# Feed-forward first layer by one level of Strassen's method, in an unrolled schedule of three groups

## The chip, the cores and the metric

The kernel runs on one core of a Trainium2 chip. Times are microseconds on the device; the metric is the median over several runs of the whole program. The profile is one further execution with the hardware profiler on.

## The reference

The reference computes one layer of a hybrid decoder in float32 for 512 prompt tokens and 32 sample tokens (544 in all, 1024 features):

```python
x = x + 0.5 * swiglu(rms_norm(x, norm_gain[l, 0]), ffn_in[l, 0], ffn_out[l, 0])
mix, st = token_mixer(rms_norm(x, norm_gain[l, 1]), ...)      # attention, pooling, caches
x = x + mix @ w_out[l]
x = x + 0.5 * swiglu(rms_norm(x, norm_gain[l, 2]), ffn_in[l, 1], ffn_out[l, 1])

def swiglu(h, w_io, w_o):
    gate, up = jnp.split(h @ w_io, 2, axis=-1)
    return (jax.nn.silu(gate) * up) @ w_o
```

`ffn_in` is 1024 x 5632 for each block: 22 tiles of 128 hidden features for the gate and as many for the up part. `ffn_out` is 2816 x 1024. The change touches these two feed-forward blocks. What lies between them (the projection with `w_in`, attention, pooling, the cache outputs, `w_out`) is computed as before.

## The kernel before, in words

Activations lie transposed: features on the partitions, the 544 tokens in the free dimension, in two halves of 272 (`HALF`). To keep float32 precision every operand of a product is split into a high part (`fp32r`, written by ScalarE with a Copy) and a low part (the remainder, a subtraction on VectorE), and `three(out, a, b)` issues three matmuls into one PSUM bank: high x high, high x low, low x high (lines 828 to 833).

A feed-forward block (`ffn(f)`, written once per engine) runs in two blocks of 11 tiles of hidden features (`BCH`). For each tile, `chunk` multiplies gate and up weights (two slots of the ring of four) with both halves of the tokens: 2 x 2 banks, 8 steps of k, 3 matmuls, 96 in all. Two sets of four banks alternate. ScalarE splits the next weights (`lead`, line 1313), applies silu to the gate banks (L1377) and writes the high part of the hidden tile (L1381); VectorE writes the weights' remainder (`remain`, L1647), multiplies silu by the up banks (L1744) and writes the hidden tile's remainder (L1734). After 11 tiles the second layer follows: 8 chunks of 128 output features, each 2 halves x 11 hidden tiles x 3 = 66 matmuls; VectorE adds half of the result to `XT` (L1763). The tiles run in hardware loops (`Fori`) on every engine.

What sets the order: each engine has its own list of instructions, written by hand, and waits on counting semaphores. `w_hi`, `w_lo` and `w_used` count weights split and weights consumed; SP loads weights into the ring when `w_used` says that a slot is free. Ahead of the first tile VectorE forms the normalised operands in pieces of 272 (`hn`, L1717, L1721), ScalarE their high parts (`parts`, L1362); TensorE begins with the first piece. In the second block of `ffn(0)` VectorE also prepares norm 1 after each chunk (L1771, L1630, L1631, L1775, L1777). GpSimd's list gathers cache pages, then issues 33 copies of cache rows from DRAM to DRAM, paced by `w_used` (L673), then computes the pooling windows (`windows`, L460 to L474) and later gathers again. It does no arithmetic in the feed-forward blocks.

Of the kernel before, what the change touches and what calls it, by code (L numbers as in the profile page):

```python
# [21 lines left out]
P = 128  # L22
# [140 lines left out]
def build(nc, I, O):  # L163
    ctx = ExitStack()
    with ctx:
# [27 lines left out]
        HIDH = put("HIDH", [P, BCH, T], "BIG", dt=F32R)  # L193
        HIDL = put("HIDL", [P, BCH, T], "BIG", BCH * T, dt=F32R)
# [44 lines left out]
        HIDF = BIG[:, BCH * T:2 * BCH * T].rearrange("p (n t) -> p n t", n=BCH)  # L239
# [23 lines left out]
        ff = [{n: sem(f"ffn{f}_{n}") for n in ("silu", "free", "mul", "hi", "lo")} for f in range(2)]  # L263
# [39 lines left out]
        CKS = CKT[:, :, :].rearrange("p b n -> p (b n)")  # L303
# [37 lines left out]
        MX1 = SM[:, 198:201]  # L341

# [141 lines left out]
        def _(sp):  # L484
# [14 lines left out]
            def chunk_loads(f, first, c, used):  # L499

                src = I["ffn_in"][0, f].rearrange("(k p) n -> p k n", p=P)
                for gs in range(2):
                    sl = (first + gs) % RING
                    if used is not None:
                        sp.wait_ge(w_used, used + gs)
                    dst = RAW[:, sl, 0:KD * P].rearrange("p (k n) -> p k n", k=KD)
                    sp.dma_start(dst, src[:, :, bass.ds(c * P + gs * FF, P)]).then_inc(landed[sl], 16)

            def ffn_loads(f):
                for blk in range(2):  # L510
# [20 lines left out]
                    src = I["ffn_out"][0, f].rearrange("(k p) n -> p k n", p=P)[:, blk * BCH:(blk + 1) * BCH, :]
                    for oc in range(KD):
                        sl = (L + oc) % RING
                        sp.wait_ge(w_used, L + oc - RING + 1)
                        sp.dma_start(RAW[:, sl, :].rearrange("p (k n) -> p k n", k=BCH),
                                     src[:, :, oc * P:(oc + 1) * P]).then_inc(landed[sl], 16)
# [109 lines left out]
        def _(pool):  # L646
# [24 lines left out]
            for dst, src, before in pieces:  # L671
                pool.wait_ge(w_used, 4 + 66 * before // copied)
# [59 lines left out]
            for b in range(2, NB):  # L732
                pool.wait_ge(sa["pva"], b - 1)
                load_slc(b)


        @block.tensor
        def _(pe):
# [102 lines left out]
            def ffn(f):  # L841
                pe.sem_inc(ff[f]["free"], 2)
                r = rs[2 * f]
                for blk in range(2):
                    L0 = L_FFN[f] + blk * L_BLOCK
                    e0 = blk * (BCH + KD)

                    def chunk(m, it, step):

                        L, e = L0 + 2 * m, e0 + m  # L850
                        pe.wait_ge(ff[f]["free"], it * step + (e + 1))
                        for hf in range(2):
                            for gs in range(2):
                                if hf == 0:
                                    pe.wait_ge(w_hi, it * (2 * step) + (L + gs + 1))
                                    pe.wait_ge(w_lo, it * (2 * step) + (L + gs + 1))
                                sl = (L0 + 2 * m + gs) % RING
                                for k in range(KD):
                                    if m == 0 and gs == 0 and blk == 0:
                                        pe.wait_ge(r["hi"], hf * KD + k + 1)  # L860
                                        pe.wait_ge(r["lo"], hf * KD + k + 1)
                                    mm = three(PS[:, 4 * (e % 2) + 2 * gs + hf, 0:HALF], weights(sl, k, (0, P), P),
                                               (HNH[:, k, halves(hf)], HNL[:, k, halves(hf)]), k == 0, k == KD - 1)
                                if hf == 1:
                                    mm.then_inc(w_used, 1)

                    with pe.Fori(0, BCH // 2) as it:
                        for u in range(2):
                            chunk(u, it, 2)
                    chunk(BCH - 1, 0, 0)  # L870
                    LO, eo = L0 + 2 * BCH, e0 + BCH

                    def out_chunk(oc, it, step, wait_last):
                        L, e = LO + oc, eo + oc
                        pe.wait_ge(ff[f]["free"], it * step + (e + 1))
                        pe.wait_ge(w_hi, it * step + (L + 1))
                        pe.wait_ge(w_lo, it * step + (L + 1))
                        sl = (LO + oc) % RING
                        for hf in range(2):
                            for n in range(BCH):  # L880
                                if wait_last and hf == 0 and n >= BCH - 2:
# [1325 lines left out]
```

## Time and profile before

| | us |
|---|---|
| median of 3 runs | 1701.4 (1700.25 to 1705.1) |
| the profiled execution's own time | 1701.34 |
| its span, first to last instruction | 1699.5 |
| TensorE busy | 1596.2 (94%) |
| VectorE busy | 815.5 (48%) |
| ScalarE busy | 656.7 (39%) |
| GpSimd busy | 121.7 (7%) |
| mean granted TensorE clock | 0.980 |

Matmuls overlap: a single one is recorded with some 0.29 us, while the next starts about 0.125 us after it. An engine's busy share is an average over stages with different limits, and a duration on GpSimd is rough. "L1647" is line 1647 of the kernel; helpers such as `lead` and `remain` have one line for all their uses.

### The profile page before, as it was taken

The page shows a single profiled execution, that of the slowest core. Times are in us where ns is not written, and L with a number is a line of the kernel's source. Part 1 is how long each engine was busy: PE and PEld are TensorE (multiplying, and loading weights), DVE is VectorE, ACT ScalarE, POOL GpSimd, SP SyncE. Part 2 cuts the span into 40 slices and gives each one's busy share as a digit, 9 for nine tenths or more (in the row PEclk, how much of TensorE's full clock was granted, in tenths as well). Part 3 has the DMA queues.
Part 4 walks back from the last instruction along what each step waited for, and adds up shares of the span by engine and source line. Part 5 has one row for each costly group of instructions (what it writes and reads, how often), then busy time and mean ns, then how long its engine had stood idle before and what let it go on. Part 6 is the DMA issues. An engine that isn't in the chain of part 4 may idle for free.

```text
span 1699.5 us, 27997 instructions
## 1 busy us (share of the span) xinstructions
PE 1596.2 (94%) x11347; PEld 1482.7 (87%) x11347; DVE 815.5 (48%) x1527; ACT 656.7 (39%) x1172; POOL 121.7 (7%) x155
## 2 busy tenths in 40 slices
PE   3999999899999999999987998999798999999998
PEld 2788887899999999999975776777697999999998
DVE  2677779633332335525647995322356333233331
ACT  1666666422213432223244554455514342122221
POOL 0000000000000000001043002333000000000000
PEclk9999999999999999999978999999899999999999
DMA  9222421244435444333134004988222233222321
GB/s 329 99 100 114 185 100 50 100 136 136 152 121 184 138 143 164 100 114 132 43 112 128 1 1 124 257 257 255 66 86 59 79 97 104 71 87 74 108 88 67
DMA packets 183689, 202.27 MB, mean 119 GB/s; under 512 B 9830, under 2 KB 167245, under 8 KB 181005
## 3 DMA queue, kind: packets, MB, share of 16 engines
q1 hardware_dynamic: 167573, 111.67, 21.7%
q0 software_dynamic: 11680, 89.10, 15.3%
q8 instruction: 58, 0.95, 0.2%
q10 hardware_dynamic: 4352, 0.34, 0.2%
q14 instruction: 26, 0.21, 0.0%
HBM read 195.86 MB, written 31.40 MB: 134 GB/s over the span
## 4 chain that ended last, share of the span: by engine, by line
PE 85%; DVE 8%; ACT 3%; DMA 2%; issue 2%; SPq 1%; POOL 0%; DVEq 0%; ACTq 0%; PEldq 0%; POOLq 0%
PE PS L831 19%; PE PS L833 19%; PE PS L832 18%; PE PS L792 3%; PE PS L793 3%; PE PS L794 3%; PE PS L778 3%; PE PS L1188 2%; PE PS L1116 1%; PE PS L1141 1%; PE PS L1164 1%; SPq L587 1%; DMA HN<-in_cmp_w 1%; PE PS L1169 1%; PE PS L1084 1%
## 5 line engine op out<-in xcount | busy, mean ns | idle before, releaser
L831 PE MATMUL PS<-HNH,WHI 128*128 128x272 f32 x1408 | 408.6, 290 | 7.8 <-DVE HNL L1721 6.8
L832 PE MATMUL PS<-HNL,WHI 128*128 128x272 f32 x1408 | 406.4, 289 | 0.0
L833 PE MATMUL PS<-HNH,WLO 128*128 128x272 f32 x1408 | 405.8, 288 | 0.0
L831 PEld LDWEIGHTS PS<-HNH,WHI 128*128 128x128 f32 x1408 | 266.7, 189 | 11.1 <-issue 8.0
L1313 ACT ACTIVATE WHI<-WR 128x1024 fp32r<-128x1024 f32 (+3 forms) x144 | 164.6, 1151 | 277.7 <-DMA WR<-in_ffn_in 127.7
L832 PEld LDWEIGHTS PS<-HNL,WHI 128*128 128x128 f32 x1408 | 267.4, 190 | 0.0
L1647 DVE TENSOR_TENSOR WLO<-WR,WHI 128x1024 fp32r<-128x1024 f32 (+3 forms) x144 | 192.4, 1343 | 156.1 <-ACT WHI L1313 155.6
L833 PEld LDWEIGHTS PS<-HNH,WLO 128*128 128x128 f32 x1408 | 267.3, 190 | 0.0
L1655 DVE TENSOR_TENSOR PT<-PS,PT 64x512 fp32r<-64x512 f32 x256 | 176.3, 689 | 61.5 <-ACT PT L1320 58.7
L831 PE MATMUL PS<-HIDH,WHI 128*128 128x272 f32 x704 | 202.4, 288 | 0.0
L833 PE MATMUL PS<-HIDH,WLO 128*128 128x272 f32 x704 | 202.4, 287 | 0.0
L832 PE MATMUL PS<-HIDL,WHI 128*128 128x272 f32 x704 | 201.9, 287 | 0.0
L1320 ACT ACTIVATE PT<-PS 64x512 fp32r<-64x512 f32 x256 | 151.9, 593 | 93.4 <-PE PS L778 91.8
L1744 DVE TENSOR_TENSOR BIG<-GB,PS 128x544 f32 (+1 forms) x44 | 31.7, 721 | 210.0 <-PE PS L833 208.3
L833 PEld LDWEIGHTS PS<-HIDH,WLO 128*128 128x128 f32 x704 | 132.5, 188 | 0.0
L832 PEld LDWEIGHTS PS<-HIDL,WHI 128*128 128x128 f32 x704 | 132.2, 188 | 0.0
L831 PEld LDWEIGHTS PS<-HIDH,WHI 128*128 128x128 f32 x704 | 132.0, 188 | 0.0
L792 PE MATMUL PS<-PT,CW1H 128*128 128x512 f32 x256 | 114.3, 446 | 1.9 <-DVE PT L1655 1.9
L793 PE MATMUL PS<-PT,CW1H 128*128 128x512 f32 x256 | 102.0, 398 | 0.0
L794 PE MATMUL PS<-PT,CW1L 128*128 128x512 f32 x256 | 101.9, 398 | 0.0
L1763 DVE SCALAR_TENSOR_TENSOR XT<-PS,XT 128x544 f32<-128x544 f32 x32 | 23.2, 725 | 158.4 <-PE PS L833 158.4
L831 PE MATMUL PS<-WHI,HNH 128*128 128x324 f32 (+1 forms) x256 | 80.3, 314 | 2.8 <-PE PS L940 2.8
(359 smaller groups left out, 2512.4 us busy)
## 6 DMA issues: line engine op xcount, KB each, us to landing
WR<-in_ffn_in SPq DMA_DIRECT2D x88, 512.0 KB, 3.7
WR<-in_ffn_out SPq DMA_DIRECT2D x32, 704.0 KB, 4.4
out_dil_s<-in_cache_dil_kv POOLq DMA_DIRECT2D x8, 2044.0 KB, 9.2
WR<-in_w_in SPq DMA_DIRECT2D x14, 648.0 KB, 4.4
BIG<-in_cache_dil_kv SPq DMA_DIRECT2D x8, 512.0 KB
WR<-in_w_out SPq DMA_DIRECT2D x8, 512.0 KB, 3.8
out_dil_s<-in_cache_dil_kv POOLq DMA_DIRECT2D x8, 508.0 KB, 5.0
out_win_s<-in_cache_win_kv POOLq DMA_DIRECT2D x8, 508.0 KB, 5.4
```

The source lines that it names most:

```text
L778: mm = pe.transpose(PS[:, 2 * (X % 2) + p, j * 256 + half * P:j * 256 + (half + 1) * P], PB[b % 2][:, half, c:c + P], ident)
L792: pe.matmul(out, hi, pt[:, 0, j, :, c:c + 256], start=(q == 0 and x == 0), stop=False)
L793: pe.matmul(out, hi, pt[:, 1, j, :, c:c + 256], start=False, stop=False)
L794: mm = pe.matmul(out, lo, pt[:, 0, j, :, c:c + 256], start=False, stop=(q == 3 and x == 3))
L831: pe.matmul(out, a[0], b[0], start=first, stop=False)
L832: pe.matmul(out, a[0], b[1], start=False, stop=False)
L833: return pe.matmul(out, a[1], b[0], start=False, stop=last)
L1188: mm = pe.matmul(out[:, t], ETA[0:R, j, :], kv[0:R, t, :, j * 256 + P:j * 256 + P + HD], start=(j == 0), stop=(j == 3))
L1313: act.activation(WHI[:, sl, 0:n], RAW[:, sl, 0:n], ACT.Copy).then_inc(w_hi, 1)
L1320: last = act.activation(PTX[X % 4][p * HD:(p + 1) * HD, 0, :, h, 0:256], PS[h * HD:(h + 1) * HD, 2 * (X % 2) + p, :].rearrange("p (j n) -> ...
L1647: V.tensor_tensor(WLO[:, sl, 0:n], RAW[:, sl, 0:n], WHI[:, sl, 0:n].bitcast(F32), ALU.subtract)\
L1655: last = V.tensor_tensor(pt[:, 1], src, pt[:, 0].bitcast(F32), ALU.subtract)
```

## The change

The 22 tiles of a block are taken in three groups of 8, 7 and 7 (`GROUPS`), each followed by 8 chunks of the second layer over the group's tiles (2 x 8 x 3 = 48 or 2 x 7 x 3 = 42 matmuls). All loops are written out. The first layer of a tile treats [gate | up] x [k low | k high] x [token half] as a 2 x 2 block product and forms it from seven products of 4 steps of k, 3 matmuls each (84), with sums of weights and sums of operands.

Who does what now:

- GpSimd: `weight_sums`, four sums of 128x512 per tile, and `hid_lo`, the remainder of the hidden tile (before on VectorE). It issues the cache copies in between.
- ScalarE: `part_hi`, seven high parts of 128x512 per tile (before two of 128x1024), a copy of product 0, silu of each token half by itself, `hid_hi`.
- VectorE: `part_lo`, seven remainders of 128x512; seven adds that put the products together (`add`); two products of 272.
- `operands(f)` replaces `hn` and `parts`: whole operands of 4 x 272, four sums of them, a high part and a remainder each. For norm 2 the reciprocal of both halves stands ahead of it.
- The ring becomes four slots of raw weights and seven slots of parts (`part_free`). The squares of the compressed keys (`ck_squares`) are formed in four pieces.

The diff's core: the parts' slots, GpSimd's list, TensorE's products, ScalarE's step, VectorE's operands and its step, in this order.

```diff
+GROUPS = ((0, 8), (8, 7), (15, 7))
+PART_SLOT = (2, 3, 4, 5, 6, 0, 1)
+PROD_B11, PROD_T1, PROD_T2, PROD_B22, PROD_T3, PROD_B21, PROD_T4 = range(7)
...
+        def part_free(engine, f, q):
+            if q >= 7:
+                engine.wait_ge(w_used, Q_FFN[f] + q - 6)
+            elif f == 1:
+                engine.wait_ge(w_used, L_OUT + (6, 6, 7, 8, 8, 8, 8)[q])
+            elif q >= 2:
+                engine.wait_ge(m_done, NCH)
...
+            def weight_sums(f, s):
+                _, _, _, _, q, u = STEPS[s]
+                done = 4 * tile_no(f, s)
+                raw_landed(pool, f, u)
+                raw_landed(pool, f, u + 1)
+                part_free(pool, f, q + 1)
+                nc.gpsimd.tensor_tensor(s1, a21, a22, ALU.add).then_inc(ff["weight_sums"], 1)
+                part_free(pool, f, q + 2)
+                pool.wait_ge(ff["weight_sums"], done + 1)
+                nc.gpsimd.tensor_tensor(s2, s1, a11, ALU.subtract).then_inc(ff["weight_sums"], 1)
+                part_free(pool, f, q + 3)
+                pool.wait_ge(ff["weight_sums"], done + 2)
+                nc.gpsimd.tensor_tensor(s4, a12, s2, ALU.subtract).then_inc(ff["weight_sums"], 1)
+                part_free(pool, f, q + 4)
+                nc.gpsimd.tensor_tensor(s3, a11, a21, ALU.subtract).then_inc(ff["weight_sums"], 1)
+            def hid_lo(f, s):
+                m = STEPS[s][3]
+                pool.wait_ge(ff["hid_hi"], tile_no(f, s) + 1)
+                nc.gpsimd.tensor_tensor(HIDL[:, m, :], HIDF[:, m, :], HIDH[:, m, :].bitcast(F32), ALU.subtract)
+            for s, (in_layer1, _, _, x, q, _) in enumerate(STEPS):
+                if in_layer1:
+                    weight_sums(0, s)
+                if s and STEPS[s - 1][0]:
+                    hid_lo(0, s - 1)
+                while (in_layer1 or x < 4) and sent < N_COPIES and spread(pieces[sent][2]) < q + 7:
+                    pool.wait_ge(w_used, max(q, 1))
+                    pool.dma_start(pieces[sent][0], pieces[sent][1]).then_inc(cpy, 16)
...
+                def product(s, j):
+                    q, t = STEPS[s][4] + j, tile_no(f, s)
+                    if s and STEPS[s - 1][0]:
+                        if j:
+                            pe.wait_ge(ff["partial"], 7 * (t - 1) + (0, 5, 1, 3, 4, 6, 7)[j])
+                        else:
+                            pe.wait_ge(ff["kept"], t)
+                    elif j in (0, 4):
+                        pe.wait_ge(bank_free[f], s + 1 + j // 4)
+                    pe.wait_ge(w_hi, Q_FFN[f] + q + 1)
+                    pe.wait_ge(w_lo, Q_FFN[f] + q + 1)
+                    for k in range(4):
+                        mm = three(PS[:, j, 0:HALF], part(q, k), (TH[j][:, k, :], TL[j][:, k, :]), k == 0, k == 3)
+                    mm.then_inc(w_used, 1)
...
+                    if in_layer1:
+                        act.wait_ge(w_used, Q + q + 1)
+                        act.activation(SUM1, PS[:, 0, 0:HALF], ACT.Copy).then_inc(ff["kept"], 1)
+                        if after_tile:
+                            hid_hi(s - 1)
+                        for j in range(4):
+                            part_hi(f, q + j + 7)
+                        act.wait_ge(ff["partial"], 7 * t + 3)
+                        act.activation(GB[:, s % 2, 1, :], SUM3, ACT.Silu).then_inc(ff["silu"], 1)
+                        for j in (4, 5):
+                            part_hi(f, q + j + 7)
+                        act.wait_ge(ff["partial"], 7 * t + 6)
+                        act.activation(GB[:, s % 2, 0, :], SUM1, ACT.Silu).then_inc(ff["silu"], 1)
+                        part_hi(f, q + 6 + 7)
...
+                for k in range(4):
+                    scaled(k)
+                sum_of(t1, b12, b11, 4)
+                rest(0, b11)
+                for k in range(4, 8):
+                    scaled(k)
+                sum_of(t2, b22, t1, 9)
+                rest(1, t1)
+                sum_of(t4, b21, t2, 10)
+                sum_of(t3, b22, b12, 10)
+                dve.wait_ge(r["f"], 12)
+                rest(2, t2)
+                rest(3, b22)
+                rest(4, t3)
+                rest(5, b21)
+                rest(6, t4)
...
+                        part_lo(f, q + 7)
+                        dve.wait_ge(ff["kept"], t + 1)
+                        add(1, SUM2, SUM1, PROD_T2, 0)
+                        part_lo(f, q + 8)
+                        add(2, SUM3, SUM2, PROD_T1, 1)
+                        add(3, SUM3, SUM3, PROD_B22, 2)
+                        part_lo(f, q + 9)
+                        add(4, SUM2, SUM2, PROD_T3, 0)
+                        part_lo(f, q + 10)
+                        add(5, SUM4, SUM2, PROD_T1, 4)
+                        part_lo(f, q + 11)
+                        add(6, SUM1, SUM1, PROD_B21, 0)
+                        part_lo(f, q + 12)
+                        add(7, SUM2, SUM2, PROD_T4, 0)
+                        dve.wait_ge(ff["silu"], 2 * t + 2)
+                        V.tensor_tensor(HIDF[:, x, HALF:T], GB[:, s % 2, 1, :], SUM4, ALU.mult)
+                        dve.wait_ge(ff["partial"], 7 * t + 7)
+                        V.tensor_tensor(HIDF[:, x, 0:HALF], GB[:, s % 2, 0, :], SUM2, ALU.mult).then_inc(bank_free[f], 1)
+                        part_lo(f, q + 13)
```

Each `add` has one input in SBUF and one in PSUM; it waits for the product (`w_used`) and, where it needs an earlier sum, for `partial`. `rest(j)` is the remainder of operand j, behind the `part_lo` of product j. A `part_hi` of products 1 to 4 waits for its weight sum. `hid_hi` waits for the tile's last product on VectorE, `hid_lo` for `hid_hi`.

## Rows read from the trace of the kernel before

**Rows 1.** The page: shares of the span, and of the chain that ended last.
```profile
PE 1596.2 (94%) x11347; PEld 1482.7 (87%) x11347; DVE 815.5 (48%) x1527; ACT 656.7 (39%) x1172; POOL 121.7 (7%) x155
PE 85%; DVE 8%; ACT 3%; DMA 2%; issue 2%; SPq 1%; POOL 0%; DVEq 0%; ACTq 0%; PEldq 0%; POOLq 0%
```
**Rows 2.** Stretches: length, busy time (instructions) of the engines in order, clock, DMA.
```profile
306.00:310.00 4.00, 3.71 (x15) 3.59 (x15) 4.00 (x12) 2.16 (x6) 0.00 (x0) 0.51 0.00 0
...
1302.00:1688.00 386.00, 386.00 (x3076) 386.00 (x3075) 117.15 (x116) 101.54 (x109) 0.00 (x0) 1.00 0.29 84
```
**Rows 3.** VectorE in time, first layer: start, duration, instruction, [idle before].
```profile
333.95 0.72 DVE L1744 TENSOR_TENSOR BIG<-GB,PS 128x544 f32 x1 [6.02 <-PE PS L833]
...
358.10 0.72 DVE L1744 TENSOR_TENSOR BIG<-GB,PS 128x544 f32 x1 [6.27 <-PE PS L833]
```
**Rows 4.** VectorE in time, the last two chunks of the first block.
```profile
699.22 0.72 DVE L1763 SCALAR_TENSOR_TENSOR XT<-PS,XT 128x544 f32<-128x544 f32 x1 [3.36 <-PE PS L833]
...
707.49 0.72 DVE L1763 SCALAR_TENSOR_TENSOR XT<-PS,XT 128x544 f32<-128x544 f32 x1 [3.36 <-PE PS L833]
```
**Rows 5.** Groups of instructions, shapes apart: busy us, mean ns of one.
```profile
L1655 DVE TENSOR_TENSOR PT<-PS,PT 64x512 fp32r<-64x512 f32 x256 | 176.3, 689 | 61.5 <-ACT PT L1320 58.7
L1647 DVE TENSOR_TENSOR WLO<-WR,WHI 128x1024 fp32r<-128x1024 f32 x96 | 116.7, 1224 | 79.9 <-ACT WHI L1313 79.4
L1313 ACT ACTIVATE WHI<-WR 128x1024 fp32r<-128x1024 f32 x96 | 100.2, 1054 | 151.4 <-DMA WR<-in_ffn_in 127.7 <-DMA WR<-in_w_out 23.5
...
L1381 ACT ACTIVATE HIDH<-BIG x40 | 26.4, 660 | 116.6 <-DVE BIG L1744 116.6
...
L1721 DVE TENSOR_TENSOR HNL<-QTR,HNH 128x272 fp32r<-128x272 f32 x32 | 13.9, 436 | 0.9
```
**Rows 6.** GpSimd in time, in the pooling windows.
```profile
878.09 1.24 POOL L474 TENSOR_TENSOR BIG<-BIG,WR 64x496 f32<-64x496 f32 x1
879.41 1.05 POOL L460 TENSOR_TENSOR BIG<-BIG 128x521 f32<-128x521 f32 x1
...
883.40 1.26 POOL L460 TENSOR_TENSOR BIG<-BIG 128x513 f32<-128x513 f32 x1
...
886.51 1.33 POOL L474 TENSOR_TENSOR BIG<-BIG,WR 64x496 f32<-64x496 f32 x1
```
**Rows 7.** VectorE in time, in the same stretch.
```profile
878.75 0.56 DVE L1910 TENSOR_TENSOR WR<-WR,PS 128x384 f32<-128x384 f32 x1 [4.11 <-PE PS L1002]
...
884.30 0.77 DVE L1916 TENSOR_TENSOR WR<-WR 128x384 f32<-128x384 f32 x1
...
886.78 1.10 DVE L476 SCALAR_TENSOR_TENSOR BIG<-BIG,CO,WR 64x32 f32<-64x32 f32 x1
...
888.38 0.25 DVE L476 SCALAR_TENSOR_TENSOR BIG<-BIG,CO,WR 64x32 f32<-64x32 f32 x1
```
**Rows 8.** All engines in time, the start of the first block.
```profile
296.85 2.35 DVE L1647 TENSOR_TENSOR WLO<-WR,WHI 128x1024 fp32r<-128x1024 f32 x2
...
303.95 0.42 DVE L1664 COPY CV<-PS 128x256 f32<-128x256 f32 x1
...
306.29 0.57 PE L831 MATMUL PS<-HNH,WHI 128*128 128x272 f32 x1 [2.55 <-DVE HNL L1721]
...
321.81 0.72 DVE L1744 TENSOR_TENSOR BIG<-GB,PS 128x544 f32 x1 [1.09 <-PE PS L833]
```
**Rows 9.** Costs of issuing on GpSimd's queue (groups), and weight loads (page, DMA issues).
```profile
L673 POOL DMA_DIRECT2D out_dil_s<-in_cache_dil_kv x24 | 11.8, 494 | 459.6 <-PE PS L833 427.9 <-PEq L947 31.7
...
WR<-in_ffn_in SPq DMA_DIRECT2D x88, 512.0 KB, 3.7
```
**Rows 10.** VectorE in time, around norm 2 and at the second block's end.
```profile
1278.99 0.72 DVE L1631 TENSOR_TENSOR GB<-GB 128x544 f32<-128x544 f32 x1
1281.80 1.85 DVE L1714 RECIPROCAL GB<-GB 128x272 f32<-128x272 f32 x1 [2.09 <-ACT GB L1336]
...
1688.35 0.72 DVE L1763 SCALAR_TENSOR_TENSOR XT<-PS,XT 128x544 f32<-128x544 f32 x1 [7.54 <-PE PS L833]
```

More of the change, by code:

```diff
@@ L262, in build @@
         rs = [{n: sem(f"rms{r}_{n}") for n in ("sq", "sum", "root", "f", "hi", "lo")} for r in range(3)]
-        ff = [{n: sem(f"ffn{f}_{n}") for n in ("silu", "free", "mul", "hi", "lo")} for f in range(2)]
+        ff = {n: sem(f"ffn_{n}") for n in ("silu", "hid_hi", "hid_lo", "kept", "partial", "weight_sums")}
+        bank_free = [sem("ffn0_banks_free"), sem("ffn1_banks_free")]
         pj_mm, pj_ev = sem("pj_mm"), sem("pj_ev")
@@ L734, in _ @@
                 load_slc(b)
+            for s in range(NSTEP):
+                if STEPS[s][0]:
+                    weight_sums(1, s)
+                if s and STEPS[s - 1][0]:
+                    hid_lo(1, s - 1)
         @block.tensor
@@ L841, in ffn @@
             def ffn(f):
[L842 removed]
+                pe.sem_inc(bank_free[f], 2)
                 r = rs[2 * f]
[L844 to L851, printed above, removed]
[L852 to L892 removed]
@@ new lines, in features @@
+                def features(s):
+                    _, first, n, oc, q, _ = STEPS[s]
+                    pe.wait_ge(bank_free[f], s + 1)
+                    if oc < 2:
+                        pe.wait_ge(ff["partial"], 7 * (FCH * f + first + n - 1) + 5 + oc)
+                    for j in range(2):
+                        pe.wait_ge(w_hi, Q_FFN[f] + q + j + 1)
+                        pe.wait_ge(w_lo, Q_FFN[f] + q + j + 1)
+                        for hf in range(2):
+                            for m in range(4 * j, min(n, 4 * j + 4)):
+                                if oc == 0 and hf == 0:
+                                    pe.wait_ge(ff["hid_hi"], FCH * f + first + m + 1)
+                                    pe.wait_ge(ff["hid_lo"], FCH * f + first + m + 1)
+                                mm = three(PS[:, 4 * (oc % 2) + hf, 0:HALF], part(q + j, m - 4 * j),
+                                           (HIDH[:, m, halves(hf)], HIDL[:, m, halves(hf)]), m == 0, m == n - 1)
+                        mm.then_inc(w_used, 1)
@@ L896, in _ @@
+                for s in range(NSTEP):
+                    if STEPS[s][0]:
+                        for j in range(7):
+                            product(s, j)
+                    else:
+                        features(s)
+                pe.wait_ge(bank_free[f], 2 + NSTEP - (f == 0))
             ffn(0)
@@ L1589, in _ @@
                 act.activation(MIXH[:, k, :], MIXT[:, k, :], ACT.Copy).then_inc(mx["hi"], 1)
-            for L in range(L_OUT + 2, L_FFN[1] + 2):
+            for L in range(L_OUT + 2, L_OUT + KD):
                 lead(L, KD * P)
+            part_hi(1, 0)
+            part_hi(1, 1)
             rms(2)
-            parts(2)
-            ffn(1, 0)
+            operands(1)
+            ffn(1)
             for x in range(1, 10, 2):
```

433 lines of the change are left out of this document (245 added, 188 removed).

## The prediction

> **What bounds the kernel now.** I read the page's shares first, then TensorE by stretches, then single instructions in time. TensorE is busy 94% of the span and holds 85% of the chain that ended last [rows 1]. Two thirds of that is the feed-forward blocks: in the second one 3076 matmuls take 386.0 us without a gap, at the full clock, 0.1255 us each [rows 2]. A first-layer tile now has 96 such matmuls: two products of one tile stand 24.15 us apart over two tiles, 12.07 us each [rows 3], and 96 x 0.1255 is 12.05. A layer-two chunk of 66 matmuls takes 8.27 us [rows 4]. So in both blocks only TensorE counts; VectorE, ScalarE and GpSimd idle most of the time, and the loops cost nothing visible.
>
> **What the change removes.** Seven products of 4 x 3 matmuls are 84 per tile instead of 96: 84 x 0.1255 = 10.54 us, 1.53 less; times 44 tiles, 67 us. Layer two keeps its 1056 matmuls a block, now in 24 steps of 6.02 (eight tiles, 48 matmuls) or 5.27 us (seven, 42). Nothing else gets shorter. The loops go too, with them the table loads inside; neither was on the path.
>
> **What it adds, per tile.** VectorE: seven part_lo (128x512, both inputs in SBUF), seven adds of 272 with one input in PSUM, two products of 272; hid_lo leaves it. GpSimd, idle so far: four weight sums of 512 and hid_lo of 544. ScalarE: one copy and two silu of 272, seven part_hi of 512, hid_hi of 544.
> Durations: a VectorE tensor_tensor takes 0.436 us at 272 and 0.689 at 512; from 272 to 1024 elements it grows 1.05 ns an element [rows 5]. Back to back the next starts some 0.09 us before that end (two L1647 of 1.224 take 2.35 together [rows 8]), so I count 0.60 at 512 and 0.355 at 272, and 0.50 where an add needs the one just before it. VectorE: 7 x 0.60 + 6 x 0.355 + 0.50 + 2 x 0.355 = 7.5 us a tile, under 10.54. ScalarE: 0.66 for hid_hi, 1.054 at 1024 elements, so 0.62 at 512 [rows 5]; together 6.3 us. GpSimd has two prices: 1.24 us at 496 and 1.26 at 513 elements, but 1.05 at 521 [rows 6]. These are 5.3 to 6.4 us a tile. Each engine alone would keep up with TensorE.
>
> **Why they don't keep up together.** One stretch has GpSimd and VectorE beside each other [rows 6, 7]. A VectorE operation of 32 elements takes 0.25 us alone and 1.10 while GpSimd's L474 runs; it ends 0.04 after it. L1916 (384 elements, some 0.56 alone) takes 0.77 and ends 0.41 after GpSimd's operation, just its own 384 elements later. L1910, with one input in PSUM, keeps its 0.56 beside L474. So a VectorE operation with two SBUF inputs and a GpSimd tensor_tensor exclude each other; the seven adds run free. The converse holds too: L474 at 886.51 took 1.33 instead of 1.24. A blocked GpSimd operation has its start-up behind it, so I count 0.13 less after the release.
>
> The order of waits now makes one chain. From the end of a tile's last product on VectorE (time 0), with TensorE ahead:
> - ScalarE hid_hi to 0.69, GpSimd hid_lo (1.33) to 2.08; part_lo of product 0 for the next tile is ready at 1.3 and blocked till 2.08: 2.63;
> - GpSimd sum 1, blocked by that: 3.76; sum 2: 5.10; part_lo for sum 1 (its part_hi is done at 4.4) blocked till 5.10: 5.65; sum 4: 6.78; part_lo: 7.33; sum 3: 8.46; part_lo: 9.01;
> - free of GpSimd: add 5, part_lo, add 6, part_lo, add 7, two products: 4 x 0.355 + 2 x 0.60 + 0.44 = 3.06: 12.07.
> TensorE, which needs add 5 of the last tile before product 1 of the next can use its bank, then waits 1.5 us a tile. A cycle of 12.07 is what a tile costs now, by chance. The bounds: with GpSimd at the 1.05 row all five operations are about 0.21 shorter, 11.0; with 0.05 us more at each of a dozen handovers, 12.7. I take 1.25 (1.33 at 544), as L474 and L460 at 513 have it; L460 at 521 reads two places 4 elements apart, which no sum here does.
> The Trainium skill's GPSIMD Engine Reference, section 3.1 (side-by-side cycle accounting), says that a two-input GpSimd body needs about 2.6 cycles an element, as both inputs come through one read port. By its 4497 ns at 2048 elements an estimate for 512 is 1.2 us, and the cycle would be 12.0; by the 521 row it would be 11.0. The trace has both rates.
> The last tile of a group has no sums beside it: 2.6 + 3.7 + 3.06 = 9.3. The first, with TensorE not yet ahead but three of its part_lo blocked, ends its products 12.8 us after it starts.
>
> **The sum, first block.** Before, the copy L1664 ends at 304.4, the first matmul is at 306.29 and the first tile's product starts at 321.81 [rows 8]; the last step's add starts at 707.49 [rows 4]. Now operands() works on whole operands, and TensorE gets nothing until the first is complete. From 304.4: four scalings of 544 (0.63 each), t1 of 1088 elements (1.2), its remainder (1.2): first matmul 309.5. Four scalings, t2, a part_lo, its remainder: 315.0. t4, t3, and five times part_lo and remainder (1.8 each, 1.8 for the third as well): 326.5. GpSimd's four sums for the second tile fall in here and each takes about 1.1 from VectorE: 331.0. VectorE has all of the first tile's adds still before it: 7.0, to 338.0.
> - Group of eight: 338.0 + 6 x 12.07 + 9.3 = 419.7; hid_hi and hid_lo 2.1: 421.8. TensorE has 33 of its layer-two matmuls behind it, 351 are left, 44.1: 465.9.
> - Groups of seven: 12.8 + 5 x 12.07 + 9.3 + 2.1 = 84.6, then 306 matmuls, 38.4: 123.0; two are 246.0: 711.9. Before, the same work was 7 x 12.07 + 42.2 = 126.7 each.
> - GpSimd also issues the cache copies, 0.49 us each [rows 9], in its queue ahead of the next sums; about six of them fall into chained tiles: +3. End 714.9 against 707.5: **7.4 later**. The copies themselves end later but wait for nobody.
> **Second block.** The reciprocal of 272 took 1.85 [rows 10]; now both halves stand before the first scaling: 1281.80 + 3.7 = 1285.5, which is 981.1 after the first block's 304.4. 711.9 + 981.1 = 1693.0. Sums 4 and 3 of the first tile start when w_out's last chunk is done, just where the squares (two SBUF inputs, L1631) lead to the norm: +1.3. 1694.3 against 1688.35 [rows 10]: **5.9 later**.
> Hidden: the weight loads (3.7 us to land [rows 9], asked for over 10 us ahead, two raw slots a tile); in the last group of the first block VectorE has 4.5 us per step of 5.27 for norm 1, tight, and at nothing; ck_squares in four pieces, 0.8 us more, has 3 steps of lead. w_in's later loads wait for the block's end, but are needed 18 us on. Projection, attention and the tail stay: zero.
> Sum: 7.4 + 5.9 = 13.3 on the profiled execution's 1701.34 us (the same as the median of the runs, 1701.4): about 1714.
>
> **Rivals.**
> 1. *GpSimd works at the rate of its 521 row.* For: nothing in the operation differs, and no row has a 512-element sum over 128 partitions from the ring. Against: the other rows of that group. 1.07 less per cycle, 16 cycles a block, 34 us; 0.2 at each group's end and start and in the operands, 6 us: 1674. It decides from a cycle of 11.7 down, that is GpSimd at 1.17: there the result turns faster. This is the other side, one mechanism.
> 2. *TensorE stays the bound.* If the exclusion is rare, because the operations shift apart, the cycle is 10.6. TensorE is done with its first tile at 328.3, then 7 x 10.6 + 48.2 + 2 x (7 x 10.6 + 42.2) = 355.2: 683.5, 24 earlier; twice: 1653. Against: the sums are packed into the middle of VectorE's work.
> 3. *The chain is longer still:* cycle 12.7 from handovers, or from TensorE's clock at the lower of its levels, 1.2 GHz, behind its longest waits: 306 to 310, behind a wait of 2.55 us [rows 8], was granted 0.51 and held 15 matmuls in 4 us [rows 2]. 32 x 0.63 = 20: 1734.
>
> **How the numbers follow.** Forecast 0.45 (its own range 1702 to 1726), rival 1 0.28, rival 2 0.10, rival 3 0.17. 0.3% is 5 us, what a measurement can tell here. Faster: rivals 1 and 2 without a little, 0.37. Same: the low edge of the forecast and the high one of rival 1, 0.11. Slower: 0.52. The range reaches over rival 1 and to rival 3: 1668 to 1735; it leaves out rival 2 and the far tails.
>
> **What would show it.** Products of neighbouring tiles on VectorE 12.1 us apart inside a group and about 9.3 to the last; 10.6 would prove rival 2. part_lo of products 1 to 3 at 0.8 to 1.2 us instead of 0.69; the adds at 0.44 throughout. GpSimd sums 1.25. TensorE waits at product 1 for an add, 1.5 us a tile, and for HIDL at each group's first chunk. First matmul of the first block near 309.5. What makes it wrong first: GpSimd's time per sum, on which 3.2 us hang for each 0.02 us.

## The result, and the profile after

| | before | after |
|---|---|---|
| median of 4 runs, us | 1700.97 (1700.25 to 1705.1) | 1752.29 (1746.98 to 1759.16) |
| profiled execution, its own time / span | 1701.34 / 1699.5 | 1752.73 / 1749.9 |
| mean granted TensorE clock | 0.980 | 0.957 |

The change makes the kernel slower: ratio 1.0299, 95% interval [1.0274, 1.0324]. The forecast was 1714 with a range to 1735, so the sign was right and the size was not: 51 us, where 13 were forecast. One execution of a version below, e_all_dve2, took 2203.8 us at a granted clock of 0.653, for which I have no cause; it is in that version's median and not in its ratio.

The page of after, against [rows 1]: busy time, TensorE and its clock in 40 slices, the chain.

```profile
PE 1565.0 (89%) x10819; PEld 1442.5 (82%) x10819; DVE 1096.9 (63%) x2115; ACT 757.1 (43%) x1508; POOL 437.1 (25%) x375
...
PE   3999998689998989999987998999796899999998
...
PEclk9999999899999999999977999999997999999999
...
PE 59%; DVE 16%; POOL 12%; issue 7%; ACT 3%; DMA 2%; SPq 0%; POOLq 0%; DVEq 0%; ACTq 0%
```

No engine but TensorE passes 63%, yet TensorE's part of the chain fell from 85% to 59%, and GpSimd, busy a quarter of the time, holds 12% of it. Who TensorE waits for (in total, times, longest):

```profile
PE PS L917 <- DVE CKT L1899: 53.9, 34, 2.6
PE PS L917 <- DVE TL L1862: 27.0, 8, 9.9
...
PE PS L917 <- POOL HIDL L737: 4.7, 4, 3.8
```

The first row is add 5, which frees the bank for product 1, in 34 of the 44 tiles; the second is the operands at the start of the blocks. One whole cycle of the second block, from product to product on VectorE (L1921, against [rows 3]); L1783 is `part_lo`, L1899 an add:

```profile
1362.93 0.43 DVE L1921 TENSOR_TENSOR BIG<-GB,BIG 128x272 f32<-128x272 f32 x1
1363.29 0.68 DVE L1783 TENSOR_TENSOR WP<-WR,WP 128x512 fp32r<-128x512 f32 x1
1364.60 1.43 DVE L1783 TENSOR_TENSOR WP<-WR,WP 128x512 fp32r<-128x512 f32 x1 [0.64 <-ACT WP L1417]
1365.95 0.43 DVE L1899 TENSOR_TENSOR BIG<-BIG,PS 128x272 f32<-128x272 f32 x1
1368.65 0.69 DVE L1783 TENSOR_TENSOR WP<-WR,WP 128x512 fp32r<-128x512 f32 x1 [2.27 <-POOL WR L727]
1369.26 0.91 DVE L1899 TENSOR_TENSOR BIG<-BIG,PS 128x272 f32<-128x272 f32 x2
1370.53 1.76 DVE L1783 TENSOR_TENSOR WP<-WR,WP 128x512 fp32r<-128x512 f32 x1 [0.36 <-POOL WR L730]
1372.22 0.42 DVE L1899 TENSOR_TENSOR BIG<-BIG,PS 128x272 f32<-128x272 f32 x1
1372.57 0.68 DVE L1783 TENSOR_TENSOR WP<-WR,WP 128x512 fp32r<-128x512 f32 x1
1373.17 0.42 DVE L1899 TENSOR_TENSOR CKT<-BIG,PS 128x272 f32<-128x272 f32 x1
...
1375.77 0.43 DVE L1921 TENSOR_TENSOR BIG<-GB,BIG 128x272 f32<-128x272 f32 x1
```

GpSimd in the same stretch: `hid_lo` (L737), then sums 1, 2, 4, 3:

```profile
1364.13 1.35 POOL L737 TENSOR_TENSOR HIDL<-BIG,HIDH 128x544 fp32r<-128x544 f32 x1 [5.22 <-ACT HIDH L1479]
1365.44 1.74 POOL L724 TENSOR_TENSOR WR<-WR 128x512 f32<-128x512 f32 x1
1367.33 1.29 POOL L727 TENSOR_TENSOR WR<-WR 128x512 f32<-128x512 f32 x1
1368.76 1.73 POOL L730 TENSOR_TENSOR WR<-WR 128x512 f32<-128x512 f32 x1
1370.45 1.29 POOL L732 TENSOR_TENSOR WR<-WR 128x512 f32<-128x512 f32 x1
```

The exclusion can be read off. The sum at 1370.45 runs its 1.29 us undisturbed, to 1371.74; the `part_lo` of 1370.53 came 0.08 later and ends at 1372.29, its own 0.55 after the sum. The sums at 1365.44 and 1368.76 were the late ones and took 1.74 and 1.73. The adds stay at 0.42. The cycle is 12.84 us.

What is new to the forecast is in two brackets. The `part_lo` at 1368.65, for sum 1, is released by L727, sum **2**, and the one at 1370.53, for sum 2, by L730, sum **4**. The code has it: `part_lo` writes over the sum's own slot, which the following sum still reads, so for j = 1 and 2 it waits for the sum behind its own. Such a `part_lo` doesn't stand blocked at the port, ready to take it over. The one for sum 1 still gets its turn, as sum 4 waits for sum 2 too and starts 0.11 us later than the `part_lo`. The one for sum 2 doesn't: sum 3 waits for no other sum and starts at 1370.45, 0.08 us ahead of the `part_lo`.

The forecast let the engines alternate (sum 2, low, sum 4, low, sum 3, low). Here they go sum 2, low, sum 4, sum 3, low, and the `part_lo` for sum 4 comes alone at 1372.57. Counted from the end of the product before (1363.36), the low part of sum 1 ends at 5.98 (forecast 5.65) and that of sum 4 at 9.89 (forecast 9.01).

### The profile page after: what moved, and what is told of

Read it like the earlier page. It is cut to its first block, busy times and chain, and to the rows that moved or that the text cites. A ratio compares the mean times of both kernels' runs of the same rounds, so it can differ in the third digit from the quotient of the medians.

```text
span 1749.9 us, 28045 instructions
## 1 busy us (share of the span) xinstructions
PE 1565.0 (89%) x10819; PEld 1442.5 (82%) x10819; DVE 1096.9 (63%) x2115; ACT 757.1 (43%) x1508; POOL 437.1 (25%) x375
## 4 chain that ended last, share of the span: by engine, by line
PE 59%; DVE 16%; POOL 12%; issue 7%; ACT 3%; DMA 2%; SPq 0%; POOLq 0%; DVEq 0%; ACTq 0%
PE PS L917 10%; PE PS L919 10%; PE PS L918 10%; DVE WP L1783 4%; POOL WR L730 4%; PE PS L878 3%; PE PS L880 3%; PE PS L879 3%; PE PS L864 3%; POOL WR L724 3%; POOL WR L727 2%; POOL HIDL L737 2%; PE PS L1272 2%; DVE BIG L1899 2%; PE PS L1225 1%
## 5 line engine op out<-in xcount | busy, mean ns | idle before, releaser
L1783 DVE TENSOR_TENSOR WP<-WR,WP 128x512 fp32r<-128x512 f32 (+1 forms) x404 | 346.0, 858 | 208.8 <-POOL WR L727 99.8
L917 PE MATMUL PS<-TH,WP 128*128 128x272 f32 x1232 | 370.4, 301 | 84.4 <-DVE CKT L1899 53.9
L1417 ACT ACTIVATE WP<-WR 128x512 fp32r<-128x512 f32 (+1 forms) x404 | 244.4, 617 | 376.9 <-PE PS L919 142.4
L919 PE MATMUL PS<-TH,WP 128*128 128x272 f32 x1232 | 366.0, 297 | 0.0
L918 PE MATMUL PS<-TL,WP 128*128 128x272 f32 x1232 | 365.3, 296 | 0.0
L917 PEld LDWEIGHTS PS<-TH,WP 128*128 128x128 f32 x1232 | 242.1, 197 | 94.7 <-DVE CKT L1899 61.2
L918 PEld LDWEIGHTS PS<-TL,WP 128*128 128x128 f32 x1232 | 242.5, 197 | 0.0
L919 PEld LDWEIGHTS PS<-TH,WP 128*128 128x128 f32 x1232 | 242.4, 197 | 0.0
L917 PE MATMUL PS<-HIDH,WP 128*128 128x272 f32 x704 | 204.2, 290 | 4.7 <-POOL HIDL L737 4.7
L919 PE MATMUL PS<-HIDH,WP 128*128 128x272 f32 x704 | 204.8, 291 | 0.0
L918 PE MATMUL PS<-HIDL,WP 128*128 128x272 f32 x704 | 204.0, 290 | 0.0
L724 POOL TENSOR_TENSOR WR<-WR 128x512 f32<-128x512 f32 x44 | 68.4, 1555 | 283.5 <-PE PS L919 159.6
L917 PEld LDWEIGHTS PS<-HIDH,WP 128*128 128x128 f32 x704 | 133.8, 190 | 5.5 <-issue 5.5
L918 PEld LDWEIGHTS PS<-HIDL,WP 128*128 128x128 f32 x704 | 133.9, 190 | 0.0
L919 PEld LDWEIGHTS PS<-HIDH,WP 128*128 128x128 f32 x704 | 133.6, 190 | 0.0
L737 POOL TENSOR_TENSOR HIDL<-BIG,HIDH 128x544 fp32r<-128x544 f32 x44 | 59.9, 1361 | 254.1 <-ACT HIDH L1479 162.8
L1899 DVE TENSOR_TENSOR BIG<-BIG,PS 128x272 f32<-128x272 f32 x264 | 112.9, 428 | 8.8 <-PE PS L919 7.2
```

The source lines that it names most:

```text
L724: nc.gpsimd.tensor_tensor(s1, a21, a22, ALU.add).then_inc(ff["weight_sums"], 1)
L917: pe.matmul(out, a[0], b[0], start=first, stop=False)
L918: pe.matmul(out, a[0], b[1], start=False, stop=False)
L919: return pe.matmul(out, a[1], b[0], start=False, stop=last)
L1417: act.activation(WP[:, sl, 0, 0:src.shape[-1]], src, ACT.Copy).then_inc(w_hi, 1)
L1783: V.tensor_tensor(WP[:, sl, 1, 0:w], src, WP[:, sl, 0, 0:w].bitcast(F32), ALU.subtract).then_inc(w_lo, 1)
```

## The experiments

Each kernel is after with the edit shown; the two with dummy work (e_dummy_tt, e_dummy_one) start from e_all_dve2. Ratios are to the kernel before, run beside it on the same chip. "Cycle" is the distance of neighbouring products inside a group, read from VectorE in time: the value that most of them have, without the last tile of a group. The first distance of a group can differ (11.3 in e_hidlo_dve, up to 12.9 in the two e_all_dve).

| label | cycle, first block | cycle, second | median, us | ratio and interval |
|---|---|---|---|---|
| after | 12.84 to 13.41 | 12.84 | 1752.3 | 1.0299 [1.0274, 1.0324] |
| e_order | 11.87 | 11.87 | 1714.4 | 1.0056 [1.0034, 1.0078] |
| e_hidlo_dve | 12.15 | 12.16 | 1714.1 | 1.0062 [1.0040, 1.0085] |
| e_nosum | 10.57 | 10.57 | 1660.5 | 0.9742 [0.9719, 0.9764] |
| e_three_dve | 11.86 | 11.86 | 1718.7 | 1.0089 [1.0069, 1.0108] |
| e_buf | 12.85 | 12.16 | 1739.2 | 1.0200 [1.0174, 1.0226] |
| e_order_buf | 11.87 | 11.87 | 1711.2 | 1.0056 [1.0038, 1.0074] |
| e_all_dve | 11.38 | 11.38 | 1693.3 | 0.9938 [0.9919, 0.9957] |
| e_all_dve2 | 10.65 | 10.65 | 1676.7 | 0.9838 [0.9810, 0.9866] |
| e_dummy_tt | 10.65 | 15.0, 14.9, 14.9 (means by group) | 1756.8 | 1.0320 [1.0293, 1.0346] |
| e_dummy_one | 10.65 | 11.96 | 1694.9 | 0.9949 [0.9937, 0.9962] |
| e_nocopies | 12.84 | 12.84 | 1774.4 | 1.0421 [1.0400, 1.0442] |

### The order of GpSimd's list: e_order

```diff
     if in_layer1: weight_sums(f, s)
-    if s and STEPS[s - 1][0]: hid_lo(f, s - 1)
+    # tile s - 2's, behind the sums of tile s; a group's last two ahead of layer two
+    if STEPS[s][0] and STEPS[s - 1][0] and STEPS[s - 2][0]: hid_lo(f, s - 2)
```

> GpSimd's order alone: a hidden tile's low part (1.36 us) goes behind the four weight sums of the tile after next, so that the first sum no longer waits for ScalarE's high part of the finished tile. Theory (GpSimd and VectorE exclude each other, and the order of the queue adds 0.78 us per tile to the exclusive work): the exclusive work stays, 4 sums of 1.28, 1.36, 7 low parts of 0.68 and 2 products of 0.43, together 12.1 us; the cycle per tile falls from 12.85 towards it, to 12.1 to 12.6, the time to 1720 to 1742 us. Rival (the wait for the finished tile is what makes the cycle long, the exclusion is mild): the cycle falls to TensorE's 10.6 to 11.5, the time below 1700. Rival (the order doesn't matter): within 3 us of 1752.

Measured: 1714.4 us, 6 under the expected band, and a cycle of 11.87, lower than both the forecast's 12.07 and the expected 12.1. I had summed the durations of VectorE's instructions (0.68) where they start every 0.60; that alone would take more off than was measured, so the sum is not a full account of this cycle. The number equals the forecast by accident, since this kernel isn't the one forecast for. GpSimd in time:

```profile
1352.16 1.40 POOL L724 TENSOR_TENSOR WR<-WR 128x512 f32<-128x512 f32 x1 [3.85 <-PE PS L926]
1353.70 1.31 POOL L727 TENSOR_TENSOR WR<-WR 128x512 f32<-128x512 f32 x1
1355.15 1.56 POOL L730 TENSOR_TENSOR WR<-WR 128x512 f32<-128x512 f32 x1
1356.67 1.74 POOL L732 TENSOR_TENSOR WR<-WR 128x512 f32<-128x512 f32 x1
1358.37 1.82 POOL L737 TENSOR_TENSOR HIDL<-BIG,HIDH 128x544 fp32r<-128x544 f32 x1
1364.03 1.39 POOL L724 TENSOR_TENSOR WR<-WR 128x512 f32<-128x512 f32 x1 [3.85 <-PE PS L926]
```

Sum 1 now waits for TensorE's product 1 alone and starts 0.17 us ahead of the tile's last product on VectorE (1352.33, which is stretched to 1.53 us by it); in after it starts 2.1 behind the end of that product. The same five operations with the same exclusion, in another order, are worth 0.97 us a tile and 38 us in all.

### The hidden tile's remainder on VectorE: e_hidlo_dve

```diff
 (VectorE)  add(1, SUM2, SUM1, PROD_T2, 0)
+           if s and STEPS[s - 1][0]: hid_lo(f, s - 1)
            part_lo(f, q + 8)
 (GpSimd)  -hid_lo(f, s - 1)
```

> The low part of a hidden tile goes from GpSimd (1.36 us) to VectorE (0.69 us); GpSimd keeps the four weight sums. Theory (exclusion): the exclusive work falls by 0.67 us to 11.4 us per tile, the cycle to 11.4 to 12.2, the time to 1695 to 1725 us. Rival (VectorE is simply short of time, being busy 63% of the span and more in the tiles): 0.69 us more on it make the cycle 13.5 and the time about 1780. Rival (the sums, not who holds the port): no change.

Measured: 1714.1 us, cycle 12.15. More work for the busier engine, and 38 us less: VectorE is not short of time. It is 0.7 below after, as expected of 0.67 less exclusive work.

### No weight sums: e_nosum

```diff
-  a11, a12, a21, a22 = ...; s1 = a21 + a22; s2 = s1 - a11; s4 = a12 - s2; s3 = a11 - a21
-  src = WPF[:, sl, 1, :]
+  src = RAWF[:, (u + (j - 1) // 2) % 4, (j - 1) % 2 * 512:(j - 1) % 2 * 512 + 512]
```

> The four weight sums are left out: products 2 to 5 take quarters of the raw weights in their place, so that the values are others; high parts, low parts, matmuls, adds and loads stay. Theory: with 5.1 us of GpSimd work per tile gone, TensorE is the bound at 84 matmuls of 0.1255 us = 10.54 us a tile; the time is 1752 less 44 x 2.3 less some 5 us of the stall and the first tile, 1640 to 1655. Rival (seven adds out of PSUM and seven low parts bound the tile on VectorE, or TensorE waits for banks): the cycle stays over 11.5 and the time over 1690.

Measured: 1660.5 us, 5.5 over the expected band; this kernel leaves the sums out and its outputs are not the layer's. The cycle is 10.57, TensorE's 84 x 0.1255. Rival 2 of the prediction, TensorE as the bound, is what the change gives without GpSimd's sums. With them go 92 of the 1752 us.

### Three of four sums on VectorE: e_three_dve

```diff
 (VectorE)  add(1, ...)
+           weight_sum(dve, V, f, s + 1, 0)
            add(2, ...)
+           weight_sum(dve, V, f, s + 1, 1)
            part_lo(f, q + 8); add(3, ...)
+           weight_sum(dve, V, f, s + 1, 2)
 (GpSimd)   sum 3 and hid_lo stay
```

> Three of the four weight sums (the chain of sum 1, 2 and 4) go to VectorE, between its adds; the independent one and the hidden low part stay on GpSimd, and the first tile of each block keeps GpSimd's sums. Theory: VectorE's own work is then 7 adds of 0.43, 7 low parts and 3 sums of 0.68 and 2 products of 0.43, 10.65 us; the exclusive work is 1.28 + 1.36 + 10 x 0.68 + 0.86 = 10.3 us; TensorE needs 10.54. The cycle is 10.7 to 11.2, the time 1655 to 1682 us, under the kernel before (1701). Rival (VectorE is the bound already, GpSimd's work costs it little): VectorE gets 2.04 us more per tile, and the time rises to 1800 or more.

Measured: 1718.7 us, a miss by 37; the direction against after was right, the cycle stuck at 11.86. VectorE in time after the last product of a tile (L1791 is `part_lo`, L416 a sum), then GpSimd:

```profile
1361.52 0.69 DVE L1791 TENSOR_TENSOR WP<-WR,WP 128x512 fp32r<-128x512 f32 x1
1362.85 1.43 DVE L1791 TENSOR_TENSOR WP<-WR,WP 128x512 fp32r<-128x512 f32 x1 [0.65 <-ACT WP L1425]
...
1366.21 1.67 DVE L1791 TENSOR_TENSOR WP<-WR,WP 128x512 fp32r<-128x512 f32 x1
```

```profile
1362.37 1.36 POOL L742 TENSOR_TENSOR HIDL<-BIG,HIDH 128x544 fp32r<-128x544 f32 x1 [6.90 <-ACT HIDH L1487]
1365.51 1.83 POOL L416 TENSOR_TENSOR WR<-WR 128x512 f32<-128x512 f32 x1 [1.78 <-PE PS L924]
```

VectorE idles 0.65 for ScalarE, which makes the hidden tile's high part first, then loses 0.75 to `hid_lo` and 0.98 to the one sum left. VectorE has about 9.2 us of its own (an estimate: 7 x 0.35 + 10 x 0.60 + 0.70), so with these 2.4 it comes to 11.5 of the 11.86. The expectation took the 10.3 us of exclusive work for the bound and left out what a queue of fixed order loses in waiting.

### Buffers for sums 1 and 2: e_buf and e_order_buf

```diff
+ if f: s1, s2 = SB2[:, 0, :], SB2[:, 1, :]        # attention's region, free in block two
- if j <= 2:
+ if j <= 2 and not f:
      dve.wait_ge(ff["weight_sums"], 4 * tile_no(f, s) + j + 1)
```

> In the second block alone sums 1 and 2 of the weights have buffers of their own, so that the low parts 1 and 2 no longer wait for the sum after theirs; the queue of GpSimd stays as it was. Theory (the forecast left out that wait, worth 0.78 us a tile): the second block's cycle is the forecast 12.07 us in place of 12.85, the first block's stays, the time falls by 19 x 0.78 = 15 us to about 1737. Rival (the queue alone, low part of the hidden tile ahead of the sums, sets the cycle): 12.85 stays in both blocks and the time is within 4 us of 1752.

> Both repairs that keep the sums on GpSimd: the hidden tile's low part behind the sums (cycle 11.87 alone) and, in the second block, buffers of their own for sums 1 and 2 (12.17 alone). Theory (what is left then is the exclusive work: 4 x 1.28 + 1.36 of GpSimd and 7 x 0.60 + 0.70 of VectorE, 11.4 us, of which adds out of PSUM lie beside GpSimd's): the second block's cycle is 11.4 to 11.9, the time 1705 to 1714, never under the kernel before. Rival (the two waits add up, 0.98 and 0.69 us): 11.2 in the second block and 1702.

Measured: 12.16 in the second block alone and 1739.2 us. This is the test of the failed step: with the wait that I overlooked taken out, the chain that I had computed runs at 12.16 against the computed 12.07 (0.68 of the 0.77 us that the forecast missed), and the first block of the same run stays at 12.85. VectorE in time:

```profile
1369.76 1.29 DVE L1786 TENSOR_TENSOR WP<-CV,WP 128x512 fp32r<-128x512 f32 x1 [1.51 <-ACT WP L1421]
1370.97 0.90 DVE L1902 TENSOR_TENSOR BIG<-BIG,PS 128x272 f32<-128x272 f32 x2
1371.78 0.97 DVE L1786 TENSOR_TENSOR WP<-CV,WP 128x512 fp32r<-128x512 f32 x1
1372.68 0.42 DVE L1902 TENSOR_TENSOR BIG<-BIG,PS 128x272 f32<-128x272 f32 x1
1373.02 1.42 DVE L1786 TENSOR_TENSOR WP<-WR,WP 128x512 fp32r<-128x512 f32 x1
```

Three blocked `part_lo` in a row: the alternation that the forecast had. Behind the better order the buffers bring next to nothing (1711.2 us, 11.87 in both blocks but for two cycles of 11.67 and 11.53 in each group of seven of the second). The two repairs don't add up: with the better order alone VectorE is already held 39.9 of 40 us (1350 to 1390 in e_order), by its own work or by GpSimd's.

### Everything on VectorE: e_all_dve and e_all_dve2

```diff
 (VectorE)  sums 1, 2, 4, 3 and hid_lo between the adds; GpSimd keeps tile 0's sums
 e_all_dve2, ScalarE:
+           part_hi(f, q + 7)
            if after_tile: hid_hi(s - 1)
-           for j in range(4): part_hi(f, q + j + 7)
+           for j in range(1, 4): part_hi(f, q + j + 7)
 e_all_dve2, VectorE, ahead of add 1:
+           dve.wait_ge(bank_free[f], 2 + s)
```

> All four weight sums and the hidden tile's low part go to VectorE; GpSimd keeps the first tile's sums of each block alone. In the run with three sums on VectorE its two-input reads follow each other every 0.60 us and its adds every 0.35 us: 7 x 0.35 + 12 x 0.60 (seven low parts, four sums, hidden low part at 0.65) + 0.70 for two products = 10.4 us. Theory (the exclusion is what costs; a 512-wide sum holds both engines for 1.28 us on GpSimd and one engine for 0.60 on VectorE): the cycle falls to 10.6 to 11.3, the time to 1662 to 1692 us, under the kernel before. Rival (VectorE's length is the bound: the run with three sums stayed at 11.87): 1.25 us more on it make 13 us a tile and about 1765.

> As the run with all on VectorE, and ScalarE makes the high part of the first part ahead of the hidden tile's high part, so that VectorE doesn't wait for it (it waited 0.65 us a tile in the run with three sums). Theory: if VectorE's queue is the bound by then, the cycle falls by 0.2 to 0.65 us, up to 25 us of the time; if TensorE is (10.57), nothing changes.

Measured: 1693.3 us, 1.3 over the band, cycle 11.38; with ScalarE's order changed 1676.7 us and 10.65, 0.73 less (expected up to 0.65). The second beats the kernel before by 1.6% (interval 1.3 to 1.9) and after by some 4.5%, by the two ratios. Forty us in the middle of the second block's first group (length, busy time of the five engines, clock), first in after, then in e_all_dve2:

```profile
1360.00:1400.00 40.00, 34.70 (x257) 34.05 (x258) 30.05 (x52) 17.46 (x34) 22.00 (x15) 0.96 0.27 80
```

```profile
1330.00:1370.00 40.00, 40.00 (x320) 40.00 (x319) 39.72 (x80) 21.51 (x42) 0.00 (x0) 1.00 0.36 106
```

In e_all_dve2 TensorE has no gap and the full clock, and VectorE is as full: 80 instructions in 39.7 us. In after it did 52 in 30.1 us, its blocked time among them, and stood idle for the rest. So both engines are at their end in e_all_dve2, and no further work fits on VectorE.

### The port by itself: e_dummy_tt and e_dummy_one

```diff
 (GpSimd, second block of e_all_dve2, from its second tile on)
+ for n in range(4):
+     pool.wait_ge(w_used, Q_FFN[1] + STEPS[s][4] + n + 1)
+     link(nc.gpsimd.tensor_tensor(SCR[:, 512:1024], SCR[:, 0:512], SCR[:, 512:1024], ALU.add))
      # e_dummy_one: nc.gpsimd.tensor_copy(SCR[:, 512:1024], SCR[:, 0:512])
```

> The better version (all on VectorE, high parts reordered; cycle 10.65 us in the second block), and in the second block, from its second tile on, GpSimd adds two scratch buffers of 512 columns four times a tile, after products 1 to 4; nobody waits for it and the outputs stay. It measures the port alone. Theory (GpSimd's two-input operations shut VectorE's two-input ones out): VectorE's queue of 10.4 us grows by up to 4 x 1.28 us, less what its adds out of PSUM (0.35 us) cover: the second block's cycle is 13 to 15 us, the first block's stays 10.65, the time rises by 19 x 2.4 to 19 x 4.4, to 1722 to 1760. Rival (it was the chain of dependences through GpSimd's slow sums): the cycle stays at 10.65 and the time at 1677.

> The same with one-input copies of 512 columns in place of the additions. Theory in its narrow form (only two-input operations of GpSimd hold the port): cycle 10.65, time within 4 us of 1677. Rival (any SBUF work of GpSimd shuts VectorE's two-input reads out): the cycle rises by four times the copy's length, as in the run with additions.

Measured: nobody waits for these operations, and the cycle goes from 10.65 to 14.9 to 15.0 us with four additions, 80 us in all. So the exclusion costs time by itself, without any dependence through GpSimd. With four copies it goes to 11.96: the narrow form of the theory is wrong, a one-input operation takes the port too. Both engines in time in e_dummy_one:

```profile
1348.76 0.43 DVE L1950 TENSOR_TENSOR BIG<-GB,CKT 128x272 f32<-128x272 f32 x1
1348.82 0.84 POOL L829 COPY CV<-CV 128x512 f32<-128x512 f32 x1 [1.83 <-PE PS L928]
1349.11 0.84 DVE L1952 TENSOR_TENSOR BIG<-GB,BIG 128x272 f32<-128x272 f32 x1
```

The product of 272, 0.43 alone, ends at 1349.95, 0.29 after the copy. Four copies (0.62 each with VectorE idle, as at 1442.10) cost 1.3 a tile and not 2.5. Over the cycle from there the four cost VectorE 0.41, 0.42 (two `part_lo` from 1349.88 on), 0.42 (a sum at 1352.48) and 0.07 (a `part_lo` at 1358.75): a copy that had to wait has part of its time behind it when it is released, and beside one of them lies an add. The Trainium skill, SBUF — State Buffer, "Who interferes with whom", says the same: a VectorE instruction with two SBUF inputs contends with a GpSimd instruction that reads SBUF, and "issue order, not op shape, decides who blocks". The rows agree on both (1.29 and 1.76 for the pair at 1370.45 and 1370.53; then 1.74 for a late sum).

### The copies moved away: e_nocopies

```diff
-  while (in_layer1 or x < 4) and sent < N_COPIES and spread(...) < q + 7:
+  while False and sent < N_COPIES and spread(...) < q + 7:
```

> All state copies go behind the first block, so that none moves data or takes GpSimd's queue in it. Theory: the one stall of the first block (a second-layer load landed late, 6.8 us) and the longer cycles with copies issued (13.4 against 12.85) go, the first block ends 7 to 9 us earlier; the stage behind it may give some back, as the copies now share the DMA engines with its loads: 1743 to 1752 us. Rival (the late load has another cause): the stall stays.

Measured: 1774.4 us. The first block does get shorter, from the first tile's last product to the last tile's 347.6 instead of 355.0 us, as expected. But the expected "may give some back" was far too small: the part between the blocks gave back 26 us, and the time is 22 over the expected band. The longest waits for `w_in` loads (total, times, longest), in after, then here:

```profile
ACT WHI L1398 <- DMA WR<-in_w_in: 31.3, 12, 3.8
```

```profile
ACT WHI L1398 <- DMA WR<-in_w_in: 79.0, 11, 35.0
```

The stall of after that this edit removes, in after:

```profile
560.71 0.63 ACT L1417 ACTIVATE WP<-WR 128x512 fp32r<-128x512 f32 x1 [4.12 <-DMA WR<-in_ffn_out]
...
561.97 1.33 POOL L737 TENSOR_TENSOR HIDL<-BIG,HIDH 128x544 fp32r<-128x544 f32 x1 [10.30 <-ACT HIDH L1479]
...
563.44 0.57 PE L917 MATMUL PS<-HIDH,WP 128*128 128x272 f32 x1 [3.82 <-POOL HIDL L737]
```

A second-layer load landed late; ScalarE took its high part ahead of the hidden tile's, so TensorE stood 3.8 us and then ran at 0.57 of its clock between 562 and 566. The gap of that group is 6.2 us longer than the same gap in the second block (60.74 against 54.55). That the copies are its cause is not shown: e_order and e_hidlo_dve keep them all and have 54.5 and 54.1 in this gap, while e_buf, whose first block has the same code as after's, has no stall there and one of some 8 us in the gap before (68.4).

## Why the prediction was wrong in size

| step of the prediction | forecast | measured |
|---|---|---|
| TensorE's gain, 84 matmuls | 10.54 a tile | 10.57 (e_nosum) |
| exclusion of the two engines, adds free | yes | yes; copies too |
| GpSimd sum / `hid_lo`, alone | 1.25 / 1.33 | 1.26 to 1.30 / 1.36 |
| first matmul; first tile's products end | 309.5; 338.0 | 309.7; 338.3 |
| **the chain, a cycle** | **12.07** | **12.84** |
| last tile of a group | 9.3 | 8.95, 8.56, 9.47 |
| from a group's last products to the next one's first | 59.0 (2.1 + 44.1 + 12.8); 53.3 | 60.1; 54.5 |
| weight loads hidden | 0 | one stall, 6.2 |
| copies in the first block | 3 | 0.56 in each of two cycles, 0.15 at most in the others |
| end of block one, later by | 7.4 | 27.9 |
| second block alone, later by | 5.9 | 22.5 |

The failed step is in the chain: it has "part_lo for sum 1 (its part_hi is done at 4.4) blocked till 5.10" and its two followers, for sums 2 and 4, stand ready and take the port at each handover. The operations and the exclusion were right; that the `part_lo` of sums 1 and 2 waits for the next sum was overlooked. The one for sum 1 so comes later, and the one for sum 2 loses its turn to sum 3. The cycle is 0.77 us longer than forecast, in 32 cycles, 26.5 us summed over all of them (14.1 in the first block with the copies' share, 12.4 in the second): about two thirds of the 38 us missed on the median. e_buf shows it for the second block, where the cycle fell by 0.68, from 12.84 to 12.16; the other 0.09 was not traced. In the first block it wasn't tried. What the prediction named as going wrong first, GpSimd's time per sum, was right within 0.05 us.

The rest, from the trace alone: 6.2 for the late load, 4.6 for four gaps between groups, each 1.1 or 1.2 longer, and 1.8 ahead of the second block. The rows after w_out, against [rows 10]:

```profile
1307.07 1.07 DVE L1746 TENSOR_TENSOR GB<-XT 128x544 f32<-128x544 f32 x1
1308.17 1.67 DVE L1747 TENSOR_TENSOR GB<-GB 128x544 f32<-128x544 f32 x1
1309.99 2.04 PE L846 MATMUL PS<-GB,CO 128*128 128x272 f32 x4 [3.78 <-DVE GB L1747]
1312.81 3.56 DVE L1867 RECIPROCAL GB<-GB 128x272 f32<-128x272 f32 x2 [2.97 <-ACT GB L1440]
```

The reciprocal starts 31.0 later than before, 3.1 more than block one's end. The two squares, beside GpSimd's sums 4 and 3, take 1.07 and 1.67 instead of 0.72 each: 1.3, just what the forecast has for them. Not in it are 0.9 that the four matmuls behind them take more (2.04 instead of 1.16, at a granted clock of 0.53 where it was 1.00 before, after TensorE had stood 3.78 us), and 0.9 that had come up before the squares and was not looked into.

The last tiles gave 1.8 back, and the 3 allowed for copies were too many. Some 2.8 us of the 37.1 between forecast and trace (50.4 later at the second block's end instead of 13.3) stay unassigned; why the gaps are longer was not tested.

Of the rivals, 1 (GpSimd at its 521 row) is refuted by the durations. 3 named a cycle of 12.7 and 1734; its size came near, but by another cause than its handovers or the clock: in after the granted clock was 0.90 from 1362.0 to 1375.8 and 1.00 from 1375.8 to 1388.6, with a cycle of 12.84 and 12.83. I also erred in taking the GpSimd order as given: putting `hid_lo` first was costed in the chain (2.08 us ahead of sum 1) but not questioned. And the range: to 1735, with a chain of a dozen cross-engine handovers in the sum, was too narrow above; each overlooked wait multiplies by 32. One side sum doesn't come out as it is printed: sums of 1.2 us make a cycle of 11.8 and not 12.0 (which takes 1.24); nothing rests on it.

## What to carry to other kernels

Work moved to an idle GpSimd is not free while VectorE reads two SBUF inputs: count both engines as one queue, where a 512-column sum costs 1.28 us on GpSimd and 0.60 on VectorE. Here all of it on the busier engine was 59 us faster than shared. Before computing a chain over two engines, list for each instruction all its semaphores, those that guard an overwrite too, and ask who already holds the port when it is released. And the order in which an engine serves two independent consumers is worth a test of its own: two such swaps gave 38 and 17 us with the same work.

## What the runs showed of the hardware that was not expected

- A GpSimd copy of 128x512 in SBUF (0.62 us alone) shuts a two-SBUF-input VectorE instruction out just as an addition does: four a tile cost 1.3 us.
- Between operations that wait for one another on GpSimd itself there is a gap of 0.14 us (1368.62 to 1368.76 in after), where independent ones overlap by 0.04 (1370.49 to 1370.45).
- In e_nocopies 27 of the 33 state copies were issued within 13 us, from 835.35 on, and the weight load issued last, by 836.0, was awaited for 35.0 us, to 876.1 (the DMA engines were 63% busy between 850 and 900, against 34% in after). That the load stood behind the copies of the other queue is the likely reading; no run separates it from other causes.
